# Two hybrid attention and delta-rule layers: the delta rule's raw blocks before the last two convolutions, and one inverse root for three tiles of queries or keys

## The reference, cut to what matters

```python
zq, zk, zv, zqkv, zg, zb, za = jnp.split(h @ lw["w_in"], SPLITS, axis=-1)
q, k, v = na_heads(zq, zk, zv, lw)            # rms_norm per head of 64, then gains
qkv = jax.nn.silu(dw_conv(zqkv, lw["gdn_conv_w"]))   # 5 taps, 12 blocks of 128 columns
q, k, v = jnp.split(qkv, 3, axis=-1)          # blocks 0-3 queries, 4-7 keys, 8-11 values
...                                            # q, k: L2-normalised, rotary for latent tokens
a_mat = jnp.where(strict, einsum(kb, k) * decay, 0.0)
t_inv = triangular_solve(eye + a_mat, eye)    # the inverse that "substitution" builds
qk = jnp.where(incl, einsum(q, k) * decay, 0.0)
u = t_inv @ (v * beta)                        # the values enter only here
```

## Time and profile before

| | us |
|---|---|
| three runs | 1377.96, 1387.01, 1393.63 |
| median | 1387.01 |
| span of the profiled execution, first to last instruction | 1390.4 |
| TensorE busy (8943 matmuls) | 1260.3 (91%) |
| VectorE busy | 573.1 (41%) |
| ScalarE busy | 310.2 (22%) |
| GpSimd busy | 90.7 (7%) |

### The profile page before, as it was taken

The page is one execution under the profiler, slowest core; times in us unless marked ns, Lnnn a source line. Parts: engine busy times, 40 slices in busy tenths (PEclk is TensorE's granted clock), DMA queues, the critical chain, the costliest instruction groups (busy, mean ns, idle before and its releaser), DMA issues.

```text
span 1390.4 us, 21245 instructions
## 1 busy us (share of the span) xinstructions
PE 1260.3 (91%) x8943; PEld 617.7 (44%) x8943; DVE 573.1 (41%) x1478; ACT 310.2 (22%) x743; POOL 90.7 (7%) x104
## 2 busy tenths in 40 slices
PE   4899996899969999999989999879798799999896
PEld 1565544575553333333346554447556233333332
DVE  1256977563442211111262687846526321212115
ACT  1237312223131010101012661222313111100000
POOL 0020011010010000000021000021000000000001
PEclk9999998999989999999999999979999899999998
DMA  9820144878566999999692012365575699999984
GB/s 340 250 77 0 61 152 125 267 253 308 207 233 226 339 400 395 400 397 396 247 350 82 0 61 84 141 175 184 199 261 194 216 315 399 398 397 400 396 328 152
DMA packets 172690, 340.86 MB, mean 245 GB/s; under 512 B 34463, under 2 KB 36903, under 8 KB 172583
## 3 DMA queue, kind: packets, MB, share of 16 engines
q1 hardware_dynamic: 164807, 312.82, 62.6%
q0 software_dynamic: 7776, 26.55, 5.2%
HBM read 318.64 MB, written 20.71 MB: 244 GB/s over the span
## 4 chain that ended last, share of the span: by engine, by line
PE 69%; DVE 14%; DMA 9%; issue 3%; SPq 3%; ACT 1%; another core or an unknown queue 1%; POOLq 0%; DVEq 0%; ACTq 0%
PE bank L514 66%; PE bank L517 3%; DVE ring L1671 3%; DVE arena L1671 3%; DMA ring<-in_moe_w_dram 3%; DMA arena<-in_moe_w_dram 2%; DVE arena L1679 1%; DMA ring<-in_w_in_dram 1%; DVE small L1679 1%; DMA arena<-tok_dram,idx 1%; ACT arena L1363 1%; SPq L1256 1%; DMA raw_dram<-ring 1%; DVE x L1679 1%; SPq L1203 1%
## 5 line engine op out<-in xcount | busy, mean ns | idle before, releaser
L514 PE MATMUL bank<-ring,arena 128*32 128x512 f32 (+1 forms) x3568 | 528.3, 593 | 15.7 <-DMA ring<-in_moe_w_dram 5.6
L514 PE MATMUL bank<-arena 128*32 128x512 f32 (+3 forms) x1680 | 363.3, 511 | 29.3 <-DVE arena L1671 20.8
L1363 ACT ACTIVATE arena<-bank 128x512 f32<-128x512 f32 (+3 forms) x320 | 143.1, 479 | 625.2 <-PE bank L517 343.0
L514 PEld LDWEIGHTS bank<-ring,arena 128*32 128x32 f32 (+1 forms) x3568 | 159.3, 114 | 241.9 <-issue 241.9
L514 PE MATMUL bank<-ring,hT 128*128 128x512 f32 x576 | 254.6, 597 | 6.0 <-DMA ring<-in_w_in_dram 4.2
L514 PEld LDWEIGHTS bank<-arena 128*32 128x32 f32 (+3 forms) x1680 | 123.1, 132 | 155.0 <-issue 117.1
L514 PEld LDWEIGHTS bank<-ring,hT 128*128 128x128 f32 x576 | 108.2, 192 | 132.3 <-issue 127.7
L1671 DVE TENSOR_TENSOR arena<-hT,bank 128x512 f32<-128x512 f32 x24 | 16.5, 688 | 347.7 <-PE bank L514 347.7
L514 PE MATMUL bank<-hT,ring 128*128 128x384 f32 x384 | 132.3, 501 | 0.0
L1671 DVE TENSOR_TENSOR arena<-bank,arena 128x512 f32<-128x512 f32 x60 | 41.5, 692 | 156.3 <-PE bank L514 144.2
L517 PE MATMUL bank<-const,arena 128*128 128x128 f32 x443 | 68.0, 288 | 35.3 <-DMA arena<-tok_dram,idx 19.6
(11 more groups left out here) (138 smaller groups left out, 867.7 us busy)
## 6 DMA issues: line engine op xcount, KB each, us to landing
ring<-in_moe_w_dram SPq DMA_DIRECT2D x72, 2048.0 KB, 16.2
ring<-in_ada_w_dram SPq DMA_DIRECT2D x24, 2048.0 KB, 9.3
arena<-in_moe_w_dram SPq DMA_DIRECT2D x24, 2048.0 KB, 15.8
ring<-in_w_in_dram SPq DMA_DIRECT2D x14, 2048.0 KB, 11.5
expert_dram<-arena SPq DMA_DIRECT2D x22, 512.0 KB, 18.1
ring<-in_w_out_dram SPq DMA_DIRECT2D x4, 2048.0 KB, 8.8
arena<-in_na_rpb_dram SPq DMA_DIRECT2D x32, 96.0 KB, 4.5
tok_dram<-arena POOLq DMA_DIRECT2D x6, 512.0 KB, 4.0
```

Of the source, the lines that this page charges most:

```text
L514: return nc.tensor.matmul(out, lhsT, rhs, start=start, stop=stop)
L1363: return nc.scalar.activation(out, in_, func, **kw)
```

## The change

- VectorE: convolution blocks 10 and 11 move behind `head_products(2)`; `lengths_and_turn(2)` follows directly on tile 1; the last two `decay_masks` come before `head_products(0)`. `qk_norm` is split into `qk_sums(which, t)` and `qk_norm(which)` over three tiles, with one inverse root of 24 columns. The queries' sums and root stand before `substitution`; the keys' sums stand at rounds 18 (two tiles) and 10 (one tile), and at round 10 their root follows.
- TensorE: `head_products(1)` and `(2)` come before `token_major(0, 1)`; `conv_cols(10)` and `(11)` and the `qk_cols` come later.
- ScalarE: its list follows the new order; the squares wait for `z_summed`.
- SyncE: `blocks_out` moves from behind the load of `win` 2 to behind that of `win` 1, thus ahead of the load of `win` 2.

```diff
 (TensorE)
                 head_products(0)
                 head_cols(2)
-                conv_cols(10)
-                token_major(0, 1)
                 head_products(1)
                 head_products(2)
-                conv_cols(11)
+                token_major(0, 1)
                 token_major(0, 2)
+                conv_cols(10)
                 arrived(pe, "win", l, 1)
                 token_major(1, 0)
+                conv_cols(11)
                 token_major(1, 1)
+                token_major(1, 2)
                 qk_cols(0, 0)
-                token_major(1, 2)
                 qk_cols(0, 1)
+                qk_cols(0, 2)
                 arrived(pe, "win", l, 2)
                 token_major(2, 0)
-                qk_cols(0, 2)
+                token_major(2, 1)
+                token_major(2, 2)
                 qk_cols(1, 0)
...
 (SyncE)
-                    if name == ("win", l, 2):
+                    if name == ("win", l, 1):
                         blocks_out()
 (ScalarE)
-                        act.wait_ge(zn_ready, 6 * l + j - 1)
+                        act.wait_ge(z_summed, 6 * l + j - 1)
...
-                    if c:
+                    if 0 < c < 11:
                         conv_silu(c - 1)
...
-                conv_back(10)
+                conv_silu(10)
                 token_tile(0, 1)
                 conv_silu(11)
+                token_tile(0, 2)
+                conv_back(10)
+                token_tile(1, 0)
                 conv_back(11)
-                token_tile(0, 2)
-                token_tile(1, 0)
...
 (VectorE)
-                    if c == 10:
                         lengths_and_turn(2)
...
+                def qk_sums(which, t):
                     dve.wait_ge(act_emptied, job["win", l, which, t])
+                    vec.reduce_sum(hss[:, t, :], sq[:, (3 * which + t) % 2, :].rearrange("p (h n) -> p h n", h=HEADS),
+                                   AX).then_inc(z_summed, 1)
+                    dve.wait_ge(z_summed, n(z_summed))
+
+                def qk_norm(which):
+                    inverse_root(flat(hr), flat(hss), 1.0 / HD)
+                    for t in range(TILES):
+                        dst3 = (z, z_k)[which][:, t, :].rearrange("p (h n) -> p h n", h=HEADS)
+                        link(tt(dst3, dst3, over(hr[:, t, :], HD)))
+                        stt(dst3, dst3, (HD ** -0.5, 1.0)[which], heads(head_g[:, l, which, :], HEADS),
+                            ALU.mult, ALU.mult).then_inc(zn_ready, 1)
...
-                        if j in (BLOCK - 2, BLOCK - 14, BLOCK // 2 - 8):
-                            qk_norm(3 + (BLOCK - 2, BLOCK - 14, BLOCK // 2 - 8).index(j))
+                        if j == BLOCK - 14:
+                            qk_sums(1, 0)
+                            qk_sums(1, 1)
+                        if j == BLOCK - 22:
+                            qk_sums(1, 2)
+                            qk_norm(1)
...
                 head_products(0)
-                qk_norm(0)
                 head_products(1)
                 vec.memset(sub_v[32:64], 0.0)
                 head_products(2)
-                qk_norm(1)
-                qk_norm(2)
+                convolve(10)
+                convolve(11)
+                for t in range(TILES):
+                    qk_sums(0, t)
+                qk_norm(0)
                 substitution()
```

More of the change, by code:

```diff
@@ L57 @@
 BIAS_ROWS = ROWS + 2
-N_SCRAP = 1040
+N_SCRAP = 1056
 ARENA = 20992
@@ L368, in program @@
         nv, ny, nt = sm(24), sm(24), sm(24)
-        hss = sm(16).rearrange("p (b n) -> p b n", b=2)
-        hr = sm(16).rearrange("p (b n) -> p b n", b=2)
+        hss, hr = smt(HEADS), smt(HEADS)
         ba, beta, decay, ga, gabs, ea = smt(16), smt(8), smt(8), smt(8), smt(8), sm(8)
@@ L402, in program @@
         x_half, x_ready, mods_ready = sem("x_half"), sem("x_ready"), sem("mods_ready")
-        zn_ready = sem("zn_ready")
+        zn_ready, z_summed = sem("zn_ready"), sem("z_summed")
         past_in, kv_stored = sem("past_in"), sem("kv_stored")
@@ L717, in _ @@
                 head_cols(2)
-                conv_cols(10)
-                token_major(0, 1)
                 head_products(1)
                 head_products(2)
-                conv_cols(11)
+                token_major(0, 1)
                 token_major(0, 2)
+                conv_cols(10)
                 arrived(pe, "win", l, 1)
                 token_major(1, 0)
+                conv_cols(11)
                 token_major(1, 1)
+                token_major(1, 2)
                 qk_cols(0, 0)
-                token_major(1, 2)
                 qk_cols(0, 1)
+                qk_cols(0, 2)
                 arrived(pe, "win", l, 2)
                 token_major(2, 0)
-                qk_cols(0, 2)
+                token_major(2, 1)
+                token_major(2, 2)
                 qk_cols(1, 0)
-                token_major(2, 1)
                 qk_cols(1, 1)
-                token_major(2, 2)
                 qk_cols(1, 2)
@@ L1494, in _ @@
                 head_cols(2)
-                conv_back(10)
+                conv_silu(10)
                 token_tile(0, 1)
                 conv_silu(11)
+                token_tile(0, 2)
+                conv_back(10)
+                token_tile(1, 0)
                 conv_back(11)
-                token_tile(0, 2)
-                token_tile(1, 0)
                 token_tile(1, 1)
-                qk_cols(0, 0)
                 token_tile(1, 2)
[L1504 to L1511, removed]
+                for t in range(TILES):
+                    qk_cols(0, t)
+                for t in range(TILES):
+                    token_tile(2, t)
+                for t in range(TILES):
+                    qk_cols(1, t)
                 b = filled("past", l)
@@ L1864, in lengths_and_turn, with convolve @@
                     ins.then_inc(gq_normed, 1)
-                for c in range(12):
+                def convolve(c):
                     acc, src = conv_acc[:, c % 2, :], conv_in[:, c % 2, :]
@@ L1878, in _ @@
                             stt(acc, src[:, tap:tap + CO], w, acc, ALU.mult, ALU.add).then_inc(conv_ready, 1)
+                for c in range(10):
+                    convolve(c)
                     if c == 1:
@@ L1886, in _ @@
                         decay_rows(c - 2)
-                    if 6 <= c < 12:
+                    if 6 <= c:
                         decay_masks(c - 6)
@@ L1894, in _ @@
                         lengths_and_turn(1)
-                    if c == 10:
                         lengths_and_turn(2)
[L1898 to L1901, removed]
+                decay_masks(4)
+                decay_masks(5)
+                def qk_sums(which, t):
                     dve.wait_ge(act_emptied, job["win", l, which, t])
[L1903 to L1907, removed]
+                    vec.reduce_sum(hss[:, t, :], sq[:, (3 * which + t) % 2, :].rearrange("p (h n) -> p h n", h=HEADS),
[3 more added lines that the diff above has]
+                    inverse_root(flat(hr), flat(hss), 1.0 / HD)
+                    for t in range(TILES):
+                        dst3 = (z, z_k)[which][:, t, :].rearrange("p (h n) -> p h n", h=HEADS)
+                        link(tt(dst3, dst3, over(hr[:, t, :], HD)))
+                        stt(dst3, dst3, (HD ** -0.5, 1.0)[which], heads(head_g[:, l, which, :], HEADS),
+                            ALU.mult, ALU.mult).then_inc(zn_ready, 1)
                 def head_products(t):
```

## The result

The changed kernel takes 1380.56 us (median; 1376.49 to 1385.37) against 1387.03 for the one before. The ratio is 0.9951, with a 95% interval of 0.993 to 0.9971: 4 to 10 us less, about 7 in the middle. The profiled span is 1379.3 us.

The account below looks back on a forecast made before the run. VectorE's substitution was taken to end 2.0 and 1.5 us behind TensorE's scores; moving the maxima 5.1 + 2.9 = 8.0 us earlier takes the median of 1387.0 to 1379 us, with a range of 1368 to 1390.

Parts of the forecast that it names:

- The bound: Before the first maxima, VectorE's substitution ends 2.0 and 1.5 us after TensorE's scores; after the change TensorE ends last.
- The sum: First maxima start 5.1 us earlier in layer 0 and 2.9 in layer 1, together 8.0 us.
- VectorE's terms: On VectorE, six roots become two of 2.5 us, blocks return earlier, and layer 0's substitution ends at 216.5, not 229.8.
- A slack of 8 us that covers all the VectorE terms above: Layer 0's substitution ends at 216.5 against scores at 224.7, so errors in VectorE's times would not matter.
- with small or no waits: In VectorE's substitution, key sums at about 194 and 202 find tiles that leave TensorE at 190 and 197.
- the root at its upper bound of 7.2: A 24-column root on VectorE costing 7.2 instead of 2.5 us would end the substitution at 226, 1 us late.
- ScalarE's new order costs nothing: Each bank ScalarE empties is asked for only three products later; for three `qk_cols` it needs 0.6 against 0.9 us each.
- The cover of the third `ada` slab: On SyncE, 1.4 us of cover in layer 1; the slab would be 0 to 4 us late, taken as 0.
- its meeting with `turns`: GpSimd's key scaling beside VectorE's `turns` costs up to 1.8 us per layer; left unchanged, a possible gain in the range.
- The slower one: Rival, chance 0.10: short waits in the head products bring half clock into the next `token_major`, 8.5 us a layer; 1396.
- The gain is swallowed: Rival, chance 0.18: third `ada` slab or inverses' queue 4 us late, or new TensorE bank waits; 0 to 4 us, 1385.
- The upper rival: Rival, chance 0.17: shorter waits keep TensorE's clock up, 3.5 us a layer, plus missed `turns` meetings; 18.6 us, 1368.

Follow-up runs that it names:

- e2: Changed kernel with only SyncE's `blocks_out` moved back behind the load of `win` 2; ratio 0.9977 to the kernel before the change.
- e1: Changed kernel with an inverse root of 8 columns for each tile again, six in a layer; ratio 1.001 to the kernel before the change.
- e7: Changed kernel with key transposes and first scores ahead of the last value product, SyncE's list unchanged; ratio 0.9981 to the kernel before the change.
- e4: Changed kernel with GpSimd's first scaling of the keys waiting for the second `turns` on VectorE; ratio 0.9935 to the kernel before the change.
- e8: As e7, but SyncE sends the inverses out and back before loading the second `ada` slab; ratio 0.991 to the kernel before the change.

## Why the prediction was right, and where a step of it failed

*The bound.* Right. VectorE was late by 2.0 and 1.5 us, and TensorE ends the stage now, with the maxima straight after the scores in both layers.

*The sum.* 5.1 + 2.9 = 8.0 predicted, 5.30 + 2.54 = 7.84 in the traces, 7 (4 to 10) in the times. For TensorE alone I had 3.1 and 1.4. From the x11 transposes to the end of the scores it was 83.04 and is 79.69 in layer 0, 3.35 less; in layer 1 80.65 and 79.57, 1.08 less. The 0.3 missing there is a wait I had not counted, 0.26 us one bank earlier in the head products (0.37 in layer 0); 0.71 at the last one is the 0.7 foreseen. Layer 0 has more than forecast all the same, since a wait that I had left out went away there, 0.45 us for a key norm before the last transpose:

```profile
224.78 1.16 PE L514 MATMUL bank<-const,arena 128*128 128x128 f32 x8 [0.45 <-DVE arena L1679]
```

The two errors have opposite signs, so the closeness of 8.0 and 7.84 is in part luck. The half clock behind the wait in layer 0 did not come back, as assumed: the mean granted clock from 156 to 200 us is 1.00, where it was 0.96.

*VectorE's terms.* A root of 24 columns takes 2.6 us (I took 2.5, with 7.2 as the bound). The substitution ends 72.3 us after the x11 transposes, where my 216.5 means 71.7. The blocks' issue on SyncE took 1.90 us and not 4.74, with no slab in front of it; in e2, behind the slab of `win` 2 again, it took 4.73.

*The step that failed.* "A slack of 8 us that covers all the VectorE terms above." The slack before the maxima is 7.4 us, but it is not the only one. I had looked at when the key tiles are ready for the sums at rounds 18 and 10, "with small or no waits", and not at who waits for the sums. ScalarE does, with a bank in its hand. The sum's own slack is much smaller: e2 moved the substitution's start from 39.25 to 43.56 us after the x11 transposes, 4.3 later, and 1.90 of it reached TensorE, which leaves some 2.4 us. Layer 1 of e2 gives the same slack (3.0 later, 0.62 of wait), and so does e1 (4.76 later, 2.34 of wait). So "with the root at its upper bound of 7.2 the end is 226, which would be 1 us late" was wrong too: the root would have moved the sum by 4.7 us, as in e1, which lost the whole gain. I likewise wrote that ScalarE's new order costs nothing since every bank is asked for only three products later. That holds for the products and not for three short transposes in a row. The forecast came out right since the changed kernel stays just inside this slack.

*SyncE.* The cover of the third `ada` slab held. In layer 1 it goes at 911.25, and the product that frees its slot ends at 911.18. With the early scores of e7 the same queue cost 10.1 us, so the danger was real, a step further on.

*GpSimd.* I had left its meeting with `turns` in the sum, and it stayed. Missing it in both layers was bounded at 3.6 us; e4's trace shows 2.8. The rule of the Trainium skill that I cited, "SBUF — State Buffer", section "Who interferes with whom", agrees with e4: with GpSimd's reading instruction moved away, both `turns` instructions last 0.42 and 0.43 us again. The other half of that rule, that the later one blocks fully, agrees with e8, where GpSimd's two instructions begin first (226.94, for 2.05 us): the first `turns` instruction (228.16, 1.12 us) ends 0.29 us behind them. In layer 0 of the changed kernel the order is not clear, as the lengthened instruction is recorded 0.12 us ahead of GpSimd's.

*The rivals.* The slower one, half clock from the short waits in the head products, did not happen: the `token_major` behind them take 13.90 us for two and 7.03 for the third, at a granted clock of 1.00. It did happen at another place, behind the third query's wait in e1 and e2. "The gain is swallowed" did not happen in the changed kernel. The upper rival was wrong on the clock. In the changed kernel it falls after 4.39 us of idle time as after 6.34; the busy times by stretch give a mean of 0.60 from 228 to 244 us, and 0.59 in the kernel before from 234 to 250:

```profile
228.00:244.00 16.00, 12.60 (x73) 7.78 (x74) 5.43 (x11) 5.11 (x18) 6.50 (x9) 0.60 0.80 142
```

Where TensorE works through that latency the clock stays up: in e7 the mean is 1.00 from 214 to 226 us, and the first probabilities' two matmuls take 0.38 us instead of 0.80.

## What to carry to other kernels

When an instruction sequence moves or gets shorter, list its outputs and ask for each who waits for it and what that engine is holding; the slack of the sequence's end says nothing of the slack of a counter in its middle. Here two small buffers tied a PSUM bank to round 18 of a solver on another engine, and 2.4 us were all there was.

A gain with two halves should be tried half by half. Here the larger reordering was not needed, since the other engine was only 2 us behind. And a step that is done earlier doesn't help while the slab behind it waits in a queue: e7 lost to SyncE's order at least what it won on TensorE, and the same step won when the queue was put in order first.

## What the runs showed of the hardware that was not expected

TensorE's clock did not follow from the length of the last wait alone. The wait of 2.09 us in the kernel before was followed by half clock in layer 0 and not in layer 1; in e1 a wait of 2.34 us in layer 0 left the next three products at 20.77 us, and one of 2.35 in layer 1 made them 22.46; in e2 1.90 us was enough in layer 0. In each of these kernels the wait has the same work on TensorE in front of it in both layers. What tells them apart no run here shows.

VectorE's two-input instruction beside GpSimd's cost VectorE 0.2 to 1.0 us on an instruction of 0.42 (0.64 to 1.46 in the changed kernel), and GpSimd only 0.2 on 2.04 for its two. Here it is VectorE's that is on the path to the next product.
